# RMSNorm statistics of the opening with tokens on partitions, in a float32 decoder layer on one TensorE

## What is computed

```python
def rmsnorm(x, g):
    x32 = x.astype(jnp.float32)
    y = x32 * lax.rsqrt(jnp.mean(x32 * x32, axis=-1, keepdims=True) + EPS)
    return (y * g.astype(jnp.float32)).astype(x.dtype)

def swiglu(x, w_gate, w_up, w_down):
    return (jax.nn.silu(x @ w_gate) * (x @ w_up)) @ w_down

x = x + 0.5 * swiglu(rmsnorm(x, ffn1_norm[l]), ffn1_w_gate[l], ffn1_w_up[l], ffn1_w_down[l])
```

## Time and profile before

| | us |
|---|---|
| median of three runs | 1718.77 |
| lowest and highest | 1718.09, 1720.46 |
| profiled execution, its own time | 1718.25 |
| its span in the trace | 1716.5 |
| PE busy in the span | 1698.9 |
| DVE busy | 1124.1 |
| ACT busy | 718.2 |
| POOL busy | 531.5 |

### The profile page before, as it was taken

One profiled execution on the slowest core, in us unless ns is written; L12 is line 12 of the kernel. 1 busy time (PEld: TensorE's weight loads), 2 busy tenths in 40 slices (PEclk: granted clock), 3 DMA queues, 4 the chain that ended last, 5 costly groups with the idle time before them and its releaser, 6 DMA issues.

```text
span 1716.5 us, 24866 instructions
## 1 busy us (share of the span) xinstructions
PE 1698.9 (99%) x8329; PEld 1385.5 (81%) x8329; DVE 1124.1 (65%) x1575; ACT 718.2 (42%) x1350; POOL 531.5 (31%) x432
## 2 busy tenths in 40 slices
PE   9999999999999999999989999999999999999999
PEld 6788888888888889887766688888888888888887
DVE  7975555555498596347888863985555555569654
ACT  5533333333344563232177832543333333334442
POOL 0454445544130141000056612145554444310000
PEclk9999999999999999999999999999999999999999
DMA  7342222233774431120100122222233322485434
GB/s 207 72 151 92 98 98 92 104 117 121 271 245 125 157 98 68 50 85 25 37 2 2 38 99 99 74 99 92 92 110 121 111 104 92 171 282 160 136 103 166
DMA packets 101694, 191.71 MB, mean 112 GB/s; under 512 B 11491, under 2 KB 13972, under 8 KB 101612
## 3 DMA queue, kind: packets, MB, share of 16 engines
q1 hardware_dynamic: 100528, 188.48, 32.4%
q0 software_dynamic: 848, 2.10, 0.9%
q10 hardware_dynamic: 236, 0.06, 0.0%
HBM read 139.74 MB, written 50.86 MB: 111 GB/s over the span
## 4 chain that ended last, share of the span: by engine, by line
PE 92%; DVE 3%; ACT 1%; POOL 1%; issue 1%; DVEq 0%; ACTq 0%
PE ps L56 29%; PE ps L57 29%; PE ps L58 29%; PE ps L1675 1%; PE ps L1603 1%; PE ps L1307 1%; ACT glu L1808 1%; POOL Pg L1975 1%; DVE loT L373 1%; PE ps L1593 1%; PE ps L1724 0%; DVE ring L502 0%; PE ps L1712 0%; PE ps L1398 0%; PE ps L1698 0%
## 5 line engine op out<-in xcount | busy, mean ns | idle before, releaser
L502 DVE TENSOR_TENSOR ring<-w_raw,ring 128x512 fp32r<-128x512 f32 x240 | 239.9, 1015 | 219.0 <-ACT ring L497 218.9
L56 PE MATMUL ps<-hiT,ring 128*128 128x512 f32 x672 | 261.5, 389 | 1.5 <-DVE ring L502 1.5
L58 PE MATMUL ps<-hiT,ring 128*128 128x512 f32 x672 | 261.5, 389 | 0.0
L57 PE MATMUL ps<-loT,ring 128*128 128x512 f32 x640 | 249.0, 389 | 0.0
L56 PE MATMUL ps<-down_ring 128*128 128x512 f32 x616 | 239.7, 389 | 0.0
L57 PE MATMUL ps<-down_ring 128*128 128x512 f32 x616 | 239.6, 389 | 0.0
L58 PE MATMUL ps<-down_ring 128*128 128x512 f32 x616 | 239.6, 389 | 0.0
L56 PE MATMUL ps<-hiB,ring 128*128 128x512 f32 x576 | 224.9, 390 | 0.0
L58 PE MATMUL ps<-hiB,ring 128*128 128x512 f32 x576 | 224.1, 389 | 0.0
L497 ACT ACTIVATE ring<-w_raw 128x512 fp32r<-128x512 f32 x240 | 150.4, 628 | 165.4 <-PE ps L58 164.0
L876 ACT ACTIVATE down_ring<-down_raw 128x512 fp32r<-128x512 f32 x176 | 109.1, 630 | 226.0 <-DMA down_raw<-act_dram 184.2
(11 more groups left out here) (259 smaller groups left out, 3004.1 us busy)
## 6 DMA issues: line engine op xcount, KB each, us to landing
down_raw<-act_dram SPq DMA_DIRECT2D x154, 256.0 KB, 2.6
w_raw<-in_w_gate SPq DMA_DIRECT2D x88, 256.0 KB, 3.0
w_raw<-in_w_up SPq DMA_DIRECT2D x88, 256.0 KB, 3.1
act_dram<-actT SPq DMA_DIRECT2D x88, 256.0 KB, 2.0
act_dram<-act SPq DMA_DIRECT2D x66, 256.0 KB, 2.0
wd<-in_w_down SPq DMA_DIRECT2D x44, 256.0 KB, 4.9
wd_mirrored<-in_w_down SPq DMA_DIRECT2D x33, 256.0 KB, 4.6
p_raw<-in_w_proj SPq DMA_DIRECT2D x15, 512.0 KB, 3.6
```

The costliest lines, as they stand in the source:

```text
L56: nc.tensor.matmul(out, w_hi, x_hi, start=first, stop=False, skip_group_check=resumed)
L57: nc.tensor.matmul(out, w_hi, x_lo, start=False, stop=False, skip_group_check=resumed)
L58: return nc.tensor.matmul(out, w_lo, x_hi, start=False, stop=last, skip_group_check=resumed)
L502: nc.vector.tensor_tensor(ring[:, e % RING, 1, :], op_source(e), ring[:, e % RING, 0, :].bitcast(F32), ALU.subtract).then_inc(op_ready, 1)
```

## The change

The sums of squares of the opening, and of it alone, are formed with tokens on the partitions. `tok_sum` takes a squared tile as the stationary operand, four blocks of 128 tokens, and one column of ones as the moving operand; the result is 128x4, four columns of one bank. Root (`tok_root`) and reciprocal (`tok_recip`) work on 128x4. `rstd_rows` spreads the result again over all partitions: four products of a column of `rstd_tok`, broadcast to 128x128, with the identity. `prep_norm` reads the spread values for B11 straight from PSUM; ACT copies the bank to `rstd` for the rest (`rstd_copy`). In half 1 the squares of tiles 4 to 7 are added to tile 3 by GpSimd (five tiles into one), so PE sums four tiles only: three ahead of the first products, the last behind units 0 and 1. The spreading of half 1 stands behind unit 2. ACT's squares of half 1 and its splits are interleaved anew. `ident` comes by ACT's queue at the start, and PE waits for it ahead of the bias product. Two semaphores of stores are made one.

```diff
 def prep_norm(dve, f, h, m):
-    if m == 0:
+    at, by = scaled_x(f, m, h), rstd[:, h * HALF:(h + 1) * HALF]
+    if f == 0 and h == 0 and m < KK:
+        by = ps[:, BANK_NORM + h, :]
+        if m == 0:
+            dve.wait_ge(rstd_step, rstd_spread(h))
+    elif m == (KK if f == 0 and h == 0 else 0):
         dve.wait_ge(rstd_ready, NHALF * 2 * f + h + 1)
...
 # head_tensor, behind units 0 and 1
+                    pe.wait_ge(squares_added, KT - ADDED - 1)
+                    tok_sum(1, ADDED, False, True).then_inc(norm_summed, 1)
...
+                    if f == 0 and u == 2:
+                        rstd_rows(pe, 1)
...
+        ADDED = 3
+        def tok_bank(h):
+            return ps[:, (BANK_WARM, BANK_NORM + 1)[h], 0:4]
+        def tok_sum(h, m, first, last):
+            for t in range(4):
+                mm = nc.tensor.matmul(tok_bank(h)[:, t:t + 1], squares[h][:, m, t * P:(t + 1) * P],
+                                      ones[:, 0:1], start=first and t == 0, stop=last and t == 3)
+            return mm
+        def rstd_rows(pe, h):
+            pe.wait_ge(rstd_step, tok_inverted(h))
+            for t in range(4):
+                mm = nc.tensor.matmul(ps[:, BANK_NORM + h, t * P:(t + 1) * P],
+                                      rstd_tok[:, 4 * h + t:4 * h + t + 1].to_broadcast([P, P]), ident[:, :],
+                                      start=True, stop=True)
+            mm.then_inc(rstd_step, 1)
+        def tok_root(act, h):
+            act.wait_ge(norm_summed, h + 1)
+            nc.scalar.activation(tok_bank(h), tok_bank(h), ACT.Sqrt, bias=eps[:, 0:1], scale=1.0 / D
+                                 ).then_inc(norm_rooted, 1)
+        def tok_recip(dve, h):
+            dve.wait_ge(norm_rooted, h + 1)
+            nc.vector.reciprocal(rstd_tok[:, 4 * h:4 * h + 4], tok_bank(h)).then_inc(rstd_step, 1)
+        def rstd_copy(act, h):
+            act.wait_ge(rstd_step, rstd_spread(h))
+            nc.scalar.activation(rstd[:, h * HALF:(h + 1) * HALF], ps[:, BANK_NORM + h, :], ACT.Copy
+                                 ).then_inc(rstd_ready, 1)
...
 # gpsimd
+            for m in range(ADDED + 1, KT):
+                pool.wait_ge(x_squared, KT + m + 1)
+                wait(pool, squares_added, m - ADDED - 1)
+                nc.gpsimd.tensor_tensor(squares[1][:, ADDED, :], squares[1][:, ADDED, :], squares[1][:, m, :], ALU.add
+                                        ).then_inc(squares_added, 1)
 # scalar
+            act.dma_start(ident[:], ident_in).then_inc(rel_bias_landed, 16)
...
             ops(0, 0, 1)
-            norm_root(act, 0, [0])
-            for m in range(KT):
+            for m in range(2):
                 square(m, 1)
+            tok_root(act, 0)
+            for m in range(2, 5):
+                square(m, 1)
+            split_hi(act, 0, "B11", 0)
+            for j in range(1, KK):
+                square(4 + j, 1)
+                split_hi(act, 0, "B11", j)
+            rstd_copy(act, 0)
             ops(0, 2, 3)
-            hi(0, "B11")
+            tok_root(act, 1)
             ops(0, 4, 5)
-            hi(0, "B21")
+            split_hi(act, 0, "B21", 0)
+            rstd_copy(act, 1)
+            for j in range(1, KK):
+                split_hi(act, 0, "B21", j)
             ops(0, 6, 7)
-            norm_root(act, 0, [1])
 # vector: tok_recip(dve, 0) for the first reciprocal; behind the first prep_norm of B21
+                    elif f == 0:
+                        tok_recip(dve, 1)
...
-                norm_recip(dve, 2 * f, [1])
+                if f == 1:
+                    norm_recip(dve, 2, [1])
 # tensor
-            sum_squares(0)
-            pe.wait_ge(rel_bias_landed, 32)
+            for m in range(KT):
+                pe.wait_ge(x_squared, m + 1)
+                mm = tok_sum(0, m, m == 0, m == KT - 1)
+            mm.then_inc(norm_summed, 1)
+            pe.wait_ge(rel_bias_landed, 48)
...
-            sum_squares(1)
+            pe.wait_ge(x_squared, KT + 1)
+            tok_sum(1, 0, True, False)
+            rstd_rows(pe, 0)
+            for m in range(1, ADDED):
+                pe.wait_ge(x_squared, KT + m + 1)
+                tok_sum(1, m, False, False)
             ffn_tensor(pe, 0)
```

More of the change, by code:

```diff
@@ L203, in build @@
                   (gate_bias[:], gate_bias_in.rearrange("n a -> a n").to_broadcast([P, P])), (gate_up_w[:], gate_up_in),
-                  (ident[:], ident_in), (head_ones[:], head_ones_in)]
+                  (head_ones[:], head_ones_in)]
         NCONST = len(consts)
@@ L214, in build @@
         x_squared, x_scaled, x_normed = [sem(n) for n in "x_squared x_scaled x_normed".split()]
+        squares_added, rstd_step = [sem(n) for n in "squares_added rstd_step".split()]
         part_added = {n: sem(f"part_added{n}") for n in ("T1", "T2", "T3", "T4")}
@@ L225, in build @@
         step_done, tile_done, down_added = sem("step_done"), sem("tile_done"), sem("down_added")
-        x_spilled = sem("x_spilled")
-        y_stored = sem("y_stored")
+        x_stored = sem("x_stored")
         def upper(t, l):
@@ L311, in prep_norm @@
         def prep_norm(dve, f, h, m):
-            if m == 0:
+            at, by = scaled_x(f, m, h), rstd[:, h * HALF:(h + 1) * HALF]
[4 more added lines that the diff above has]
+            elif m == (KK if f == 0 and h == 0 else 0):
                 dve.wait_ge(rstd_ready, NHALF * 2 * f + h + 1)
-            at, by = scaled_x(f, m, h), rstd[:, h * HALF:(h + 1) * HALF]
             if f == 0 and h == 0 and m < KK:
@@ L371, in split_lo @@
                 if f == 1:
-                    dve.wait_ge(x_spilled, 16 * 2 * KT)
+                    dve.wait_ge(x_stored, 16 * 2 * KT)
             nc.vector.tensor_tensor(part_lo_of(f, r, j), part_source(f, r, j), part_hi_of(f, r, j).bitcast(F32), ALU.subtract
@@ L440, in head_silu @@
             if f == 1:
-                act.wait_ge(x_spilled, 16 * 2 * KT)
+                act.wait_ge(x_stored, 16 * 2 * KT)
             nc.scalar.activation(at[:], ps[:, pair_bank(h, a, 0), :], ACT.Silu).then_inc(silued, 1)
@@ L1102, in norm_sum, with tok_inverted, rstd_spread @@
                                  start=True, stop=True).then_inc(norm_summed, 1)
+        ADDED = 3
+        def tok_inverted(h):
+            return 2 * h + 1
+        def rstd_spread(h):
+            return 2 * h + 2
+        def tok_bank(h):
[23 more added lines that the diff above has]
+                                 ).then_inc(rstd_ready, 1)
         def norm_sum_out(pe, h):
@@ L2146, in spill_x @@
             sp.wait_ge(out_added, i + 1)
-            sp.dma_start(x_dram[m * P:(m + 1) * P, h * HALF:(h + 1) * HALF], part(xT, m, h)).then_inc(x_spilled, 16)
+            sp.dma_start(x_dram[m * P:(m + 1) * P, h * HALF:(h + 1) * HALF], part(xT, m, h)).then_inc(x_stored, 16)
         def y_sync(sp):
@@ L2151, in y_sync @@
                 sp.wait_ge(down_added, x_final(1, m, h))
-                sp.dma_start(out[m * P:(m + 1) * P, h * HALF:(h + 1) * HALF], part(xT, m, h)).then_inc(y_stored, 16)
-            sp.wait_ge(y_stored, 16 * 2 * KT)
+                sp.dma_start(out[m * P:(m + 1) * P, h * HALF:(h + 1) * HALF], part(xT, m, h)).then_inc(x_stored, 16)
+            sp.wait_ge(x_stored, 16 * 4 * KT)
         block = ctx.enter_context(nc.Block())
@@ L2283, in prep @@
                     ops(0, 1)
-                    norm_recip(dve, 0, [0])
-                if f == 0:
+                    tok_recip(dve, 0)
                     for j in range(KK):
```

## The result

The changed kernel takes 1728.17 us (median of 5 runs, 1726.87 to 1728.77), the kernel before in the same runs 1718.77 (1718.09 to 1720.91): ratio 1.0051, 95% interval 1.0040 to 1.0062. That is 9.4 us more, slower beyond the 0.2% that can be told from no change. 1724.7 was forecast, with 1728.3 as the upper end. The profiled execution has a span of 1726.4 us, 9.9 more than before's 1716.5.

The account below looks back on a forecast made before the run. TensorE's stream was taken as the bound. At T1, PE's shift of 7.3 less the 1.7 slack gave 5.6, DVE's 5.9 was later; 1718.77 + 5.9 = 1724.7 us, range 1717.8 to 1728.3.

Parts of the forecast that it names:

- upper end: Whole kernel: range to 1728.3 us; earlier fall ends the sums 1.9 later, low clock of twice the length costs 1.7 again: +9.5.
- forecast case: Opening: clock falls under one-column products, passes slow to 0.21 us, later start carries to the end: +5.9 us, chance 55%.
- The fall: Opening's sums: granted clock drops to 0.50 at 9.25 us, 3.85 us after the first one-column pass.
- The pace: One-column passes at 1.2 GHz: 0.21 us each, against 0.109 at full clock.
- rival 2: Opening: clock falls but little lands on the path, +0.9 to +2.6 us, 1719.7 to 1721.4; chance 22%.
- rival 1: Opening: clock stays up, not slower, 0 to -1.9 us, 1716.9 to 1718.9; chance 19%.
- Up to the first unit: PE's opening: sums, bias product, tile 0, spreading and two tiles put the first unit at 23.5 us, 2.7 later than 20.8.
- Units 0 and 1: First products of B11: 5.45 us and 1.7 more for 3.4 us of low clock, ending at 30.65.
- GpSimd's additions, covered: Half 1's squares: four additions of 1.7 us each end at about 27.5 and are covered.
- The wait at unit 4: First unit on B21: PE waits 1.25 us as ACT stands at rstd_copy; unit 4 at 39.1, 7.3 later.
- DVE the later: At T1: DVE's shift of +5.9 us exceeds PE's 5.6 after slack, so DVE sets the end.
- Carried to the end: Behind T1: PE has no wait the change touches, so the shift of +5.9 us reaches the end at full size.

Follow-up runs that it names:

- e5: Changed kernel with the token sums' moving operand as all 128 columns of ones instead of one: 1719.12 us, ratio 0.9997 to the kernel before.
- e1: Changed kernel with the spreading of half 1 issued behind unit 2 of B11 only, not again in B12: 1729.05 us, ratio 1.0065 to the kernel before.
- e4: Changed kernel with ACT's copy of half 1's spread values moved behind the splits of B21: 1725.23 us, ratio 1.0033 to the kernel before.
- e2: Changed kernel with two 128-column dense products after each of the first seven tiles of half 0: 1735.58 us, ratio 1.0104 to the kernel before.
- e9: Kernel before with 128 instead of one moving column in the memory tokens' sums (line 1395): 1717.82 us, ratio 0.9986 to the kernel before.
- e10: Changed kernel with one 512-column dense product after each of the first seven tiles of half 0: 1729.36 us, single run, beside 1718.04 of the kernel before.
- e6: Changed kernel with the edits of e5, e1 and e4 together: 1719.01 us, ratio 0.9996 to the kernel before.
- e7: The kernel of e6 with half 0 also spread ahead of the tiles of half 1: 1718.86 us, ratio 0.9993 to the kernel before.

## Why the prediction was right, and where its sum was short

The mechanism was that of the forecast case: the clock fell under one-column products with TensorE never idle, and what followed ran at half speed up to the middle of B11. e5 shows that it carries the loss. The time came 3.5 us above the forecast, 0.1 below the upper end of the range, and that it stayed inside is partly luck. The upper end was made of an earlier fall and a low clock twice as long over B11. Of the excess only 1.6 us came by these two terms (0.85 and 0.7 below); a second spreading, 0.9, and a fall of the clock in the attention part, 1.8 in the profiled execution, neither of them in the sum, brought the rest. By its steps:

- **The fall.** Taken at 9.25 from the earlier trace rows; it came at 8.82. In e1 and e4, with the same opening up to there, it lay at 9.85 and 9.15, in e2 at 8.33: where exactly it falls differs by execution. Right.
- **The pace.** 0.21 taken from the earlier trace rows; from start to start a pass takes 0.213 in the low stretch and 0.112 ahead of it. Right, and it was the choice between the forecast and rival 2. The Trainium skill (TensorE: Matmul & The Clock Gate, LDWEIGHTS) gives the load's time by its columns alone, without the clock. The trace disagrees: the loads of these passes take 0.19 us ahead of the fall and 0.33 behind it. No idle gaps between bursts, the advice of the Trainium skill (TensorE: Matmul & The Clock Gate, Why this matters for your kernels), stood behind rival 1; the windows show a fall without a gap, so here it was not enough.
- **Up to the first unit.** Sums to 16.1 (15.4 forecast), bias product to 17.5 (16.7), tile 0 to 19.2 (18.4), spreading to 21.1 (20.1), first unit 24.35 (23.5). Most of the 0.85 arises in the first step, 0.7: by the fall 30 passes were done and not 35, which makes five more slow ones, 0.5, and each of the 64 took 0.003 longer than in the sum, 0.2. The other steps kept their terms within 0.1 to 0.2.
- **Units 0 and 1.** The term that was mis-sized: 1.7 for a low clock of 3.4 us, as in the earlier trace rows. It stayed low for 4.9 us of B11 and cost 2.4, 0.7 more.
- **GpSimd's additions, covered.** Right: its last three end at 27.94, and the tile that they feed is summed at 32.23.

```profile
23.27 4.67 POOL L2265 TENSOR_TENSOR squares<-squares 128x512 f32<-128x512 f32 x3 [3.87 <-ACT squares L2292]
```

- **The wait at unit 4.** 1.25 forecast against the pace of the stream, 1.3 measured the same way (1.04 in the row), released by DVE as told; e4 takes it away. Right. Unit 4 came at +9.0 instead of +7.3, nearly all of it by the 0.85 up to the first unit and the 0.7 of units 0 and 1.
- **The step that was missing.** The prediction didn't read from the loop that the spreading of half 1 is issued again in B12. 0.9 us, shown by e1's trace.
- **DVE the later.** Wrong. DVE's addition moved 7.5 (83.67 against 76.16), and PE arrives at T1 with no idle time, 8.4 later. The missing 0.9 lies on PE only and the slack of 1.7 no longer sufficed. By PE the forecast's own terms gave +5.6; 0.9 for the spreading, and 1.7 more at unit 4, make 8.2 of the 8.4.
- **Carried to the end.** 8.4 at T1 and 8.1 near 870 us: right. The last 1.8 of the profiled execution come with a clock fall in the attention part. The trace of before has none there; that of e9, which is before with the memory's norm changed, has one at 867.6 to 871.0, so it doesn't need the change.
- **Rival 1** would have been close if the clock had stayed up: e5 has the first unit at 17.85 (17.1 to 17.4 told) and unit 4 at 32.85 (31.3 to 33.3), but +0.5 at T1 where 0 to -1.9 was told: without the second spreading's 0.9 it would have been inside.

What stays open: why the clock falls near 870 us in some executions and for 3.4 or 6.8 us; how much dense work among one-column products holds it in the opening; and by what the chip tells one column from 128, of which these runs show only the effect.

## What to carry to other kernels

Where a matrix product serves only to sum over partitions, count the passes, not the columns: one column costs the time of 128 here, and a few us of it leave the clock at half for the dense work behind it, so fill the moving side to 128 columns, which cost 3.73 us for 3.63. Read the granted clock behind every stretch of thin products, even where TensorE shows no gap. And read a condition inside a loop for each value of the loop's variable: here `u == 2` held twice.

## What the runs showed of the hardware

- At the same clock, 32 one-column passes took 3.63 us and 32 of 128 columns 3.73 (e9): 127 more columns are nearly free, and with them the clock stayed up. 64 one-column passes took 10.74 us in after, most of them at 1.2 GHz, 64 of 128 columns 7.41 in e5.
- At the very start the clock column shows 1.00 while the 20 warm-up passes of 128 columns take 4.54 us, some 0.2 each, the pace of 1.2 GHz elsewhere. In e1 the one-column passes too start at 0.21, up to 6.4 us, and go on at 0.11. The clock shown for the first microseconds isn't the one they ran at.
- The time of a run follows its mean granted clock. In the 62 runs of before whose clock is on record, from the comparisons with e1 to e10 on three chips:

| mean clock | runs | us | median |
|---|---|---|---|
| 1.000 | 6 | 1716.6 to 1717.9 | 1717.3 |
| 0.999 | 26 | 1717.9 to 1719.4 | 1718.4 |
| 0.998 | 17 | 1719.9 to 1721.0 | 1720.4 |
| 0.997 | 8 | 1720.9 to 1721.5 | 1721.2 |
| 0.996 | 5 | 1723.3 to 1724.3 | 1723.5 |

The groups hardly overlap. 3.4 us at half clock lower the mean by 0.001 and cost some 1.7 us, so low stretches that come and go, like those near 870, can make most of the spread of one kernel; where they lie in these runs only a trace would show. Six runs have a mean of 1.000, which leaves no room for 3.4 low microseconds (an estimate from the rounding): the fall behind the memory's norm doesn't come in every execution either. Against this spread a gain of 1 or 2 us in the opening shows in T1's start in the trace long before it shows in a median, as e1, e6 and e7 did.
